# GpSimd makes the low part of one of an item's twelve weight units instead of the Vector engine

## The reference

```python
def expert_block(args):
    tok, g, e = args
    xb = h_pad[tok]
    gu = xb @ w_gate_up[e] + b_gate_up[e]
    gate, up = jnp.split(gu, 2, axis=-1)
    gate = jnp.minimum(gate, SWIGLU_LIMIT)
    up = jnp.clip(up, -SWIGLU_LIMIT, SWIGLU_LIMIT)
    act = (up + 1.0) * (gate * jax.nn.sigmoid(SWIGLU_ALPHA * gate))
    y = act @ w_down[e] + b_down[e]
    return y * g[:, None].astype(y.dtype)
```

## Time and profile before

| what | value |
|---|---|
| median of 3 runs | 2417.93 us (2413.48 to 2419.61) |
| profiled execution, its own time | 2426.88 us |
| its span in the trace | 2424.9 us |
| PE busy | 2191.2 us, 90% of the span |
| DVE busy | 1662.0 us, 69% |
| ACT busy | 1291.1 us, 53% |
| POOL busy | 320.5 us, 13% |
| mean granted TensorE clock | 0.957 of full speed |

### The profile page before, as it was taken

One profiled execution on the slowest core, in us unless ns is written; L12 is line 12 of the kernel. 1 busy time (PEld: TensorE's weight loads), 2 busy tenths in 40 slices (PEclk: granted clock), 3 DMA queues, 4 the chain that ended last, 5 costly groups with the idle time before them and its releaser, 6 DMA issues.

```text
span 2424.9 us, 35184 instructions
## 1 busy us (share of the span) xinstructions
PE 2191.2 (90%) x10770; PEld 1803.0 (74%) x10771; DVE 1662.0 (69%) x1803; ACT 1291.1 (53%) x1460; POOL 320.5 (13%) x305
## 2 busy tenths in 40 slices
PE   6999878799299998999998999999999999999991
PEld 5889645599287877877786777778888777888770
DVE  4311257645468768679967899997777898777772
ACT  5111257623256546567746677765555676555552
POOL 1000000002302002112212122121111122100100
PEclk8999969999599999999999999999999999999995
DMA  5111200143469669689968999997777999767744
GB/s 186 53 53 41 99 1 1 60 142 104 157 205 325 221 192 336 236 263 349 367 208 295 331 352 356 346 369 244 234 230 230 333 359 329 230 229 263 248 121 156
DMA packets 265843, 536.67 MB, mean 221 GB/s; under 512 B 14802, under 2 KB 31468, under 8 KB 265780
## 3 DMA queue, kind: packets, MB, share of 16 engines
q1 hardware_dynamic: 248884, 487.94, 57.6%
q0 software_dynamic: 16896, 47.83, 8.4%
HBM read 498.97 MB, written 36.75 MB: 221 GB/s over the span
## 4 chain that ended last, share of the span: by engine, by line
PE 54%; DVE 15%; issue 12%; ACT 4%; DMA 1%; ACTq 1%; DVEq 0%; POOL 0%; SPq 0%; POOLq 0%
PE ps L669 50%; DVE slots_between L1508 3%; DVE w_lo L1508 2%; DVE last_slot L1508 2%; ACT hT_hi L1120 2%; PE ps L886 1%; DVE work L1570 1%; DVE work L1363 1%; PE ps L809 1%; DVE region_mem L1559 1%; DVE work L1552 1%; PE ps L893 1%; DVE hT_lo L1523 1%; DVE mem_there L1513 1%; ACT hT_lo L1164 1%
## 5 line engine op out<-in xcount | busy, mean ns | idle before, releaser
L669 PE MATMUL ps<-hT_hi,hT_lo 128*128 128x512 f32 (+1 forms) x4304 | 1401.2, 390 | 12.5 <-DVE hT_lo L1533 12.5
L669 PEld LDWEIGHTS ps<-hT_hi,hT_lo 128*128 128x128 f32 x4304 | 810.0, 189 | 183.3 <-DVE w_lo L1508 18.4
L1120 ACT ACTIVATE hT_hi<-weight_ring 128x2048 fp32r<-128x2048 f32 x417 | 789.1, 1916 | 248.2 <-PE ps L669 202.7
L1508 DVE TENSOR_TENSOR slots_between<-weight_ring,hT_hi 128x2048 fp32r<-128x2048 f32 x245 | 553.7, 2287 | 76.2 <-ACT hT_hi L1120 72.2
L669 PE MATMUL ps<-slots_between,hT_lo 128*128 128x512 f32 x1344 | 528.3, 393 | 0.0
L1508 DVE TENSOR_TENSOR w_lo<-weight_ring,hT_hi 128x2048 fp32r<-128x2048 f32 x140 | 319.6, 2283 | 33.6 <-ACT hT_hi L1120 33.6
L669 PE MATMUL ps<-w_lo,hT_lo 128*128 128x512 f32 (+1 forms) x896 | 336.1, 375 | 0.0
L669 PEld LDWEIGHTS ps<-slots_between,hT_lo 128*128 128x128 f32 x1344 | 254.9, 190 | 54.7
L669 PEld LDWEIGHTS ps<-w_lo,hT_lo 128*128 128x128 f32 x896 | 168.8, 188 | 30.5
L591 POOL DMA_INDIRECT residual_rows<-work,idx_now x48 | 115.5, 2406 | 482.4 <-ACT work L1177 296.4
L669 PE MATMUL ps<-mem_there,pick 128*128 128x512 f32 x288 | 124.9, 434 | 48.7 <-issue 29.9
(11 more groups left out here) (250 smaller groups left out, 2454.1 us busy)
## 6 DMA issues: line engine op xcount, KB each, us to landing
weight_ring<-in_w_gate_up SPq DMA_DIRECT2D x280, 1024.0 KB, 7.7
weight_ring<-in_w_down SPq DMA_DIRECT2D x140, 1024.0 KB, 5.8
weight_ring<-in_w_mix_in SPq DMA_DIRECT2D x10, 1024.0 KB, 5.7
weight_ring<-in_x SPq DMA_DIRECT2D x8, 512.0 KB, 8.9
weight_ring<-in_w_mix_out SPq DMA_DIRECT2D x4, 1024.0 KB, 5.1
work<-in_x SPq DMA_DIRECT2D x8, 512.0 KB, 5.1
residual_rows<-work SPq DMA_DIRECT2D x8, 512.0 KB, 3.8
normed_rows<-work SPq DMA_DIRECT2D x8, 512.0 KB, 4.5
```

Source lines behind the costliest of these rows:

```text
L669: return pe.matmul(o, l, r, start=first, stop=last)
L1120: act.activation(w_high_part(u), ring[:, home(u), :], ACT.Copy).then_inc(s["w_high_made"], 1)
L1508: dve.tensor_tensor(w_low_part(u), ring[:, home(u), :], w_high_part(u).bitcast(f32), ALU.subtract)\
```

## The change

POOL makes the low part of unit 6, with the same subtraction. DVE leaves it out. PE waits for POOL's count at unit 6 and for DVE's count, now eleven for an item, at the others.

```diff
+POOL_UNIT = 6
...
                 with pool.If(size_now > 0):
+                    pool.wait_ge(s["w_high_made"], it * 12 + (POOL_UNIT + 1))
+                    pool.sem_inc(s["pool_waited"], 1)
+                    pool.tensor_tensor(w_low_part(POOL_UNIT), ring[:, home(POOL_UNIT), :], w_high_part(POOL_UNIT).bitcast(f32),
+                                       ALU.subtract).then_inc(s["w_low_pool"], 1)
                     with pool.If(size_far > 0):
                         pool.wait_ge(s["idx_in"], it * 16 + 48)
...
-                pe.wait_ge(s["w_low_made"], it * 12 + (u + 1))
+                if u == POOL_UNIT:
+                    pe.wait_ge(s["w_low_pool"], it + 1)
+                else:
+                    pe.wait_ge(s["w_low_made"], it * 11 + (u + (1 if u < POOL_UNIT else 0)))
...
                 products(it, 0, kinds)
-                low_unit(it, 6)
                 low_unit(it, 7)
```

More of the change, by code:

```diff
@@ L281, in hymba_kernel @@
             "bias_gu_in", "bias_d_in", "bias_gu_high", "bias_d_high", "bias_gu_low", "bias_d_low",
-            "w_high_made", "w_low_made", "rest_made", "sum_made", "w_used", "gate_read", "up_read", "sig_made", "silu_made", "a_made",
+            "w_high_made", "w_low_made", "w_low_pool", "rest_made", "sum_made", "w_used", "gate_read", "up_read", "sig_made", "silu_made", "a_made",
             "a_turned", "a_high", "a_low", "y_made", "pe_item", "act_item", "dve_item",
```

## The result

The changed kernel takes 2672.6 us (median of 4 runs, 2670.7 to 2685.2) against 2415.7 us of the kernel before (4 runs, 2412.3 to 2419.6): ratio 1.1083, interval 1.1058 to 1.1108, so 257 us slower. The forecast was 2633 us, with a range of 2570 to 2685. The profiled execution took 2674.2 us with a span of 2672.4; that of before had 2424.9, so the two traces differ by 247.5 us. That is less than 257, since the profiled execution of before took 2426.9 us and not 2415.7.

A forecast was written before the change was run, and what follows sets the result against it. PE was taken to bound FS and FF items, and PE, DVE and DMA all closely F items. Terms by kind of item sum to 215 us on the profiled 2426.9, 2642; less 9 for the median, 2633 us, range 2570 to 2685.

The forecast's parts named there:

- POOL's place on its queue: Head of POOL's pass: POOL arrives 2.5 us behind the list's issue, so PE starts unit 6 10.8 us later.
- The length: POOL's subtraction of 128x2048 for unit 6 takes 4.4 us, between 2.29 and 5.7.
- The relief: PE's waits at units 8 to 10: DVE's dropped subtraction gains 1.8 us per F item, nothing in FS and FF.
- The clock: Behind PE's pause at unit 6 the lower clock costs 2.1 us, bounds 0 and 4.2; 40 us in all.
- F behind FF: F items 4, 7 and 12, each behind an FF item: 8.8 us more each, 26 us together.
- F behind FS: F items 1, 25 and 32, each behind an FS item: 13.2 us more each, 40 us together.
- Item 34: The last item, which loads no list: 1 us more.
- Items 5 and 13: F items behind an F item, with PE pausing over 5 us at the start: 2.2 us more each, 4 together.
- F behind F: 13 F items like item 17, each behind an F item: 11.1 us more each, 144 us together.
- Is POOL free to read then?: Step on DVE's two-input work holding POOL's subtraction in F items: it ends as POOL arrives, so nothing was added.
- The rival of a subtraction held up by DVE: POOL's subtraction is held by DVE or slower than 4.4 us: 44 us more in 19 items, 2677 us; chance 0.07.
- The shorter chain of scatters: Rival: in longer items scatters land sooner; if all by 7 us, 133 us less, 2500 us; chance 0.10.

The follow-up runs named there:

- no_low6: The kernel before, but nobody makes unit 6's low part and PE multiplies with the high part again: 2379.5 us, ratio 0.9849.
- unit10: The changed kernel, but POOL makes the low part of unit 10 instead of unit 6, at the same place of its queue: 2432.6 us, ratio 1.0070.
- early6: The changed kernel, but POOL makes unit 6 for the next item between the first scatter's issue and its landing: 2463.3 us, ratio 1.0190.
- window7_half: The changed kernel, but POOL makes only unit 7's second half for the next item, behind the second scatter's issue, DVE the rest: 2393.0 us, ratio 0.9921.

## Why the prediction was right, and what was too small

**POOL's place on its queue.** Right. In item 17 POOL arrives 2.7 us behind the list (forecast 2.5), and unit 6 starts 10.9 us later than before (10.8); the mean of the 13 is 11.20. That this is the cause is shown from three sides: the same instruction for unit 10 costs 18 us and not 257, an arrival 4.4 us sooner takes 4.0 us off the F item, and the same work for unit 7, placed where POOL is in time, makes the kernel faster. The delay repeats and isn't caught up, as forecast.

**The length.** 4.4 us were taken between bounds of 2.29 and 5.7; it is 4.49 where nothing disturbs it. The figure of the Trainium skill (GPSIMD Engine Reference, section 3.1), 4497 ns, was the better one; the trace agrees with it.

**The relief.** Forecast 1.8 us in every F item; no_low6 has 1.53 in an F item behind an F item, 2.2 behind an FS item and 0.2 behind an FF item. The waits at units 8 and 9 are gone from item 17 and 0.55 is left at unit 10 (forecast 0.6).

**The clock.** Forecast 2.1, found 1.67 in the mean of the 13 (1.0 in item 17) and 2.2 to 2.3 in the means of the F items behind FS and FF items, where the granted clock was 0.50 to 0.56 in the 5 us behind the pause. So a pause of 10 to 15 us cost some 2 us behind it, like the 5.23 us of the earlier trace rows (2.1 us), as forecast. For the 13 the terms 11.20 - 1.53 + 1.67 make the 11.34 us that the item grew by; this is no check of them, as the 1.67 is what was left. Forecast was 11.1: the parts were off by 0.3 to 0.4 each, and nearly cancel, which is luck.

**The sum.** One share in it is misstated: without the clock's 40 us the 215 leave 175 and not "180 and more".

**Where 32 of the 247 us were missed.**
- *F behind FF*, 11 us: 12.4 and not 8.8 an item. Unit 6 started 10.5 us later and not 8.5: in items 7 and 12 the subtraction took 5.43 and 6.65 us, held by DVE, and before the change item 12 had begun unit 6 1.6 us sooner into the item than item 4, from which the 8.5 was read. On top came 2.0 and not 0.3, since the relief of 1.8 was taken from item 17 and these items had only 0.2 to give.
- *F behind FS*, 6 us: unit 6 started 15.2 us later and not 12.9, since POOL's copy of the index list, ahead of the subtraction, was held too. POOL's timeline of item 25, which begins at 2059.79, and DVE's:

```profile
2080.99 2.21 POOL L653 COPY idx_now<-idx_next 128x4 f32<-128x4 f32 x1 [6.06 <-DMA residual_rows<-work,idx_now]
...
2085.16 0.79 POOL L582 DMA_DIRECT2D idx_far<-expert_lists  x1 [1.36 <-issue]
```

```profile
2080.86 2.29 DVE L1517 TENSOR_TENSOR w_lo<-weight_ring,hT_hi 128x2048 fp32r<-128x2048 f32 x1 [1.11 <-ACT hT_hi L1129]
```

  Low 8 starts 0.13 us ahead of the copy, which then takes 2.21 us instead of 0.19. The list goes out 25.4 us into the item, 2 later than before, when low 8 had been elsewhere.
- *Item 34*, 6 us: it was costed at 1 because it loads no list. That was no reason: its subtraction is late all the same, and PE waits 5.8 us.
- *Items 5 and 13*, 5 us: in item 5 the pause at the start is gone, and unit 6 waits 12.0 us instead. Only the sum of the two, 6.4 us, was more than the 2.2.
- *F behind F*, 3 us, above.

So the missing 32 us have two sources. The step named "Is POOL free to read then?" added nothing: it was right for item 17, the one item whose rows it was read from, and wrong in the items whose scatters land at another moment (6 us behind FS items, some 3 behind FF items). The rival of a subtraction held up by DVE (44 us more) was there in part: it came on top of the forecast, in some items. Most of the rest comes from figures of item 17 and item 4 taken for items of another kind (the relief, the start of unit 6 in item 12), from item 34, put at 1 without a reason, and from the pause in item 5 that did not come.

**DVE.** Its busy time fell by 45 us and not by 80. 25 us of the difference are its products with both inputs in SBUF, which are longer where they meet POOL's subtraction (61.3 and 56.8 us in the forms of 128 rows against 52.7 and 53.3 before, 16.6 and 21.0 in those of 64 rows against 12.2 each). DVE's groups by form (busy us, mean ns), against 0.68 us for each of the same shapes before:

```profile
L1568 DVE TENSOR_TENSOR region_mem<-work,region_mem 128x512 f32<-128x512 f32 x78 | 61.3, 794 | 0.0
...
L1586 DVE SCALAR_TENSOR_TENSOR work<-work,region_mem 64x512 f32<-64x512 f32 x18 | 21.0, 1166 | 0.0
```

The longer products cost PE next to nothing: FS and FF items keep their length, and in F items they fall into PE's pause ahead of unit 6. The shorter chain of scatters, the largest rival, did not come: the scatter of item 17 lands 8.3 us behind its issue's end (8.4 before), with the DMA share down from 1.04 to 0.82.

## What to carry to other kernels

Before work goes to an engine with idle time, read when that engine comes to the place where the instruction is to stand, and when its reader wants the result: GpSimd was idle for more than four fifths of the span (busy 13%), and that was worth nothing here, since its queue stood behind landings of DMAs. Then look at what DVE runs in those microseconds, since in all these traces a GpSimd instruction that reads SBUF and a DVE one with two SBUF inputs take turns, down to the smallest copy, and the hold moves from item to item. And read a forecast's terms in an item of each kind, not in one. Half the work, in DVE's own gap and ahead of the wait for the last landing, brought 0.8% where the whole, at the wrong place, cost 11%.

## What was not expected of the hardware

- **The hold goes both ways, and can cost the whole of the other's instruction.** A DVE product of 0.68 us took 5.11, a low part of 2.29 took 4.90, POOL's subtraction of 4.49 took up to 7.19, and a copy of 4 columns 2.21. DVE's steps with an input in PSUM were not held (1512.70 and 1513.90 in unit10). The Trainium skill (SBUF — State Buffer, section Who interferes with whom) states this exclusion; the runs agree. Nor did POOL get in between two DVE instructions that stand back to back: in item 2 of the changed kernel it is released inside the second product (803.29), and still begins only behind the low part that DVE starts at 803.74 (806.02 + 4.46 = 810.48). That uses up what PE had in hand there: POOL ends at 810.48 and PE starts unit 6 at 810.53, 0.1 us later into the item than before. POOL's and DVE's timelines:

```profile
803.29 7.19 POOL L628 TENSOR_TENSOR slots_between<-weight_ring,hT_hi 128x2048 fp32r<-128x2048 f32 x1 [1.93 <-ACT hT_hi L1129]
```

```profile
802.53 1.29 DVE L1586 SCALAR_TENSOR_TENSOR work<-work,region_mem 128x512 f32<-128x512 f32 x2
803.74 2.28 DVE L1517 TENSOR_TENSOR last_slot<-weight_ring,hT_hi 128x2048 fp32r<-128x2048 f32 x1
```

- **A pause of PE at the start of items 5 and 13 that belongs to no engine.** In the trace of before PE's timeline has

```profile
944.28 0.79 PE L669 MATMUL ps<-mem_there,pick 128*128 128x512 f32 x1 [5.29 <-issue]
...
1329.79 0.79 PE L669 MATMUL ps<-mem_there,pick 128*128 128x512 f32 x1 [5.23 <-issue]
```

  Both are there in unit10 too, one of them in the changed kernel (item 13, 4.67 us) and in early6 (item 5), and none in the other five. These items then take 37 to 38 us where nothing else delays them, and not 44.8. What the traces add is that each of these pauses goes with loads of the program's own instructions: in the window 1324:1330 of before the table of DMA queues has two packets of 16 KB on the queue of kind "instruction", and two in 938.5:944.5; in no_low6, which has no pause there, it has none in the same place. It is so in all nine traces: two such packets in the 8 us ahead of the first matmul at each pause of some 5 us, none at the start of items 5 and 13 where the pause is missing, and one at the pauses of some 2 us at the start of items 4, 7, 12 and 34. (Item 1 has one too, without a pause of PE; the records do not say for which engine a load is.) That PE waits for its instructions fits all this, but no change tried it, and why items 5 and 13 need the loads in some executions only stays open. It does not carry the verdicts: 1.07 us for each of 16 F items, those behind an F or an FS item, are 17 us of the 20 that window7_half gained in the medians. It may be why the profiled execution of before stands 9 us above its median, which is only argued.
